# A two-block transformer kernel: the first norm's conditioning by halves of the features, GpSimd's share of the S5 turns, and the first half tile of the gated unit inside S5's last wait

## The reference, cut to what matters

```python
hl = modulate(rms_norm(xl, g_mix_norm[l]), sh1, sc1)      # h * (1 + sc1) + sh1
pl = hl @ wl                                              # 1024 -> 2048: q, k, v, fourier
...                                                       # attention, fourier mix, routed experts
```

```python
u = h @ w_in                                              # 1024 -> 1024
bu = einsum('btgh,gph->btgp', u_blk, b_bar)               # complex, 64 groups x 64 states
_, hs = associative_scan(_s5_combine, (a_elems, bu), axis=1)
y = einsum('btgp,ghp->btgh', hs, c_mat).real + d * u
g = gelu(y)
val, gate = split(g @ w_glu + b_glu, 2)                   # the gated unit, 1024 -> 2048
return val * sigmoid(gate)
```

## Time and profile before

| | us |
|---|---|
| median of 3 runs (2205.2 to 2207.2) | 2206.32 |
| the profiled execution, its own time | 2203.61 |
| its span in the profile | 2201.5 |
| TensorE busy | 2114.5 (96%) |
| VectorE busy | 1220.8 (55%) |
| ScalarE busy | 699.4 (32%) |
| GpSimd busy | 146.0 (7%) |

### The profile page before, as it was taken

One profiled execution on the slowest core, in us unless ns is written; L12 is line 12 of the kernel. 1 busy time (PEld: TensorE's weight loads), 2 busy tenths in 40 slices (PEclk: granted clock), 3 DMA queues, 4 the chain that ended last, 5 costly groups with the idle time before them and its releaser, 6 DMA issues.

```text
span 2201.5 us, 24790 instructions
## 1 busy us (share of the span) xinstructions
PE 2114.5 (96%) x9898; PEld 1424.2 (65%) x9898; DVE 1220.8 (55%) x1749; ACT 699.4 (32%) x1055; POOL 146.0 (7%) x149
## 2 busy tenths in 40 slices
PE   7999898998999899999999999999999999999997
PEld 3444444333333336678888888878777788888886
DVE  1875843344433336896665564576985646343434
ACT  4123422110111107223242232256884424232321
POOL 0011000003300023001000000000110000000000
PEclk9999999999999999999999999999999999999999
DMA  9754355999999992225454545324442222222221
GB/s 389 269 197 143 115 234 199 425 427 425 426 427 426 426 409 89 77 68 203 160 175 160 181 152 181 129 75 126 125 154 77 96 96 77 96 95 95 95 96 57
DMA packets 112679, 433.26 MB, mean 197 GB/s; under 512 B 7854, under 2 KB 13106, under 8 KB 98888
## 3 DMA queue, kind: packets, MB, share of 16 engines
q1 hardware_dynamic: 92872, 360.02, 42.8%
q0 software_dynamic: 19712, 71.93, 9.1%
HBM read 429.13 MB, written 6.36 MB: 198 GB/s over the span
## 4 chain that ended last, share of the span: by engine, by line
PE 59%; PEld 14%; DVE 8%; DMA 7%; issue 6%; ACT 3%; DVEq 2%; SPq 0%; POOLq 0%; PEldq 0%; POOL 0%; ACTq 0%
PE PS L1140 7%; PE PS L752 6%; PE PS L756 6%; PE PS L755 6%; PE PS L852 5%; DMA work<-in_w_dn 4%; PEld PS L752 4%; PEld PS L756 4%; PEld PS L755 4%; PE PS L1163 4%; PE PS L1407 3%; PE PS L1411 3%; PE PS L1410 3%; PE PS L982 2%; PE PS L1177 2%
## 5 line engine op out<-in xcount | busy, mean ns | idle before, releaser
L756 PE MATMUL PS<-work_f32r,work_f32r 128*128 128x512 f32 x1168 | 454.4, 389 | 0.0
L752 PE MATMUL PS<-work_f32r,work_f32r 128*128 128x512 f32 x768 | 299.5, 390 | 2.1 <-DVE work_f32r L2931 1.1
L755 PE MATMUL PS<-work_f32r,ring_f32r 128*128 128x512 f32 x768 | 298.8, 389 | 0.0
L2150 DVE TENSOR_TENSOR ring_f32r<-ring,work_f32r 128x2048 fp32r<-128x2048 f32 x100 | 227.7, 2287 | 125.5 <-ACT work_f32r L1561 125.0
L1561 ACT ACTIVATE work_f32r<-ring 128x2048 fp32r<-128x2048 f32 x100 | 190.3, 1910 | 305.8 <-DMA ring<-in_mlp_w 248.8
L756 PEld LDWEIGHTS PS<-work_f32r,work_f32r 128*128 128x128 f32 x1168 | 219.2, 188 | 45.7
L1140 PE MATMUL PS<-work 128*64 128x512 f32 x752 | 170.6, 597 | 2.2 <-ACT work L1756 2.2
L752 PEld LDWEIGHTS PS<-work_f32r,work_f32r 128*128 128x128 f32 x768 | 144.2, 188 | 33.0 <-DVE work_f32r L2931 1.5
L755 PEld LDWEIGHTS PS<-work_f32r,ring_f32r 128*128 128x128 f32 x768 | 144.2, 188 | 30.1 <-issue 0.2
L752 PE MATMUL PS<-h_f32r,work_f32r 128*128 128x512 f32 x400 | 156.0, 390 | 1.2 <-DVE work_f32r L2170 1.2
L755 PE MATMUL PS<-h_f32r,ring_f32r 128*128 128x512 f32 x400 | 155.6, 389 | 0.0
(11 more groups left out here) (440 smaller groups left out, 3334.8 us busy)
## 6 DMA issues: line engine op xcount, KB each, us to landing
work<-in_w_gu SPq DMA_DIRECT2D x47, 2048.0 KB, 21.2
ring<-in_mlp_w SPq DMA_DIRECT2D x64, 1024.0 KB, 5.2
work<-in_w_dn SPq DMA_DIRECT2D x24, 2048.0 KB, 24.4
ring<-in_w_gu SPq DMA_DIRECT2D x16, 2048.0 KB, 23.9
work<-in_ada_w_2T POOLq DMA_DIRECT2D x16, 1536.0 KB, 6.8
ring<-in_m_w_in SPq DMA_DIRECT2D x20, 1024.0 KB, 5.2
work<-in_w_adaT POOLq DMA_DIRECT2D x8, 2048.0 KB, 10.7
work<-in_ada_w_2T POOLq DMA_DIRECT2D x32, 512.0 KB, 3.6
```

What stands on the lines that cost most here:

```text
L752: mm = nc.tensor.matmul(PS[:, bank + k, :], f32r(w_of), f32r(hi(c)), start=first and c == 0, stop=False)
L755: nc.tensor.matmul(PS[:, bank + k, :], f32r(wlo), f32r(hi(c)), start=False, stop=False)
L756: mm = nc.tensor.matmul(PS[:, bank + k, :], f32r(w_of), f32r(lo(c)), start=False, stop=last and c == 3)
L2150: tt(f32r(ring[:, s, at, :]), ring[:, s, at, :], f32r(tiles[s][:, at, :]), ALU.subtract).then_inc(w_split, 1)
```

## The change

It has three parts.

**Front.** The columns of `w_ada` are reordered outside the kernel, so that one part of 2 MB holds four row chunks of one half of the features (shift and scale). SyncE's order becomes: part 0, part 1 (first half of the features), half the projection tile, part 2, part 3, the other half. TensorE conditions the first half of the features, turns it, starts the projections chunk by chunk with four of them side by side, and does the conditioning of the second half between chunks. The first norm's sum is joined on VectorE (`add_square`) and needs two chunks on TensorE. One `modulation` and two evacuations move ahead.

**S5.** VectorE keeps the doublings n = 1 to 8; GpSimd does n = 16 (two calls), then 32 and 64 for one quad at a time, with a semaphore for each quad. VectorE takes two of the four lag copies. TensorE's order gets turns of powers between the projections and loses four `keep_warm` calls.

**Gated unit.** The first half tile (48 matmuls) is issued in pieces around `states_to_outputs(7)`, and its weights are split on VectorE ahead of quad 7.

```diff
@@ SyncE, front
-            for q in range(4):
-                sp.dma_start(w_early[q], rows(A["w_ada"])[:, 2 * q:2 * q + 2, :]).then_inc(in_mod[q], 16)
-            load_tile(0, 0, 0, columns(A["w_in"]))
+            for q in range(4):
+                load_early(q)
+                if q % 2:
+                    half = q // 2
+                    sp.dma_start(ring[:, 0, 4 * half:4 * half + 4, :], rows(A["w_in"])[:, 4 * half:4 * half + 4, 0:TN]) \
+                        .then_inc(tile_loaded[half], 16)
@@ relay
-                    sp.wait_ge(bu_and_t_mm, 2 * (k - 1))
+                    sp.wait_ge(bu_and_t_mm, within_in(k - 2))
@@ GpSimd
-            pool.wait_ge(mod_mm, 1)
+            pool.wait_ge(mod_mm, COND)
+            pool.wait_ge(in_mod[3], 16)
...
+            def turn_doubled(n, first, count):
...
+                for k in range(2):
+                    ptt(dst[k], turn_c[:, part, 0:n], by[k], ALU.mult)
+                    ptt(made[k], turn_s[:, part, 0:n], by[1 - k], ALU.mult)
+                pool.drain()
+                ptt(dst[0], dst[0], made[0], ALU.subtract)
+                pool_step(ptt, dst[1], dst[1], made[1], ALU.add)
+            pool.wait_ge(s5_angles_set, 2)
+            for first in (0, 16):
+                turn_doubled(16, first, 16)
+            for q in range(KC):
+                for n in (32, 64):
+                    turn_doubled(n, 4 * q, 4)
+                pool.sem_inc(s5_set, 1)
@@ TensorE, front
-            norm_sum(0, h, T)
...
+            pe.wait_ge(in_x, 16)
+            keep_warm(3, 10)
+            pe.wait_ge(cond_ready, 1)
+            condition(0)
+            first_norm_sum()
+            keep_warm(3, 4)
+            condition(1)
+            first_spread_out()
+            conditions_turned(0)
+            keep_warm(3, 6)
...
+            for c in range(KC):
+                if c % 4 == 0:
+                    pe.wait_ge(tile_loaded[c // 4], 16)
+                pe.wait_ge(h_ready, c + 1)
+                for e in range(4):
+                    if c == 3 and e == 2:
+                        conditions_turned(1)
+                    mm = nc.tensor.matmul(PS[:, e, :], ring[:, 0, c, e * P:(e + 1) * P], h[:, c, :], start=(c == 0), stop=(c == KC - 1))
...
+                if c == 1:
+                    condition(2)
+                elif c == 2:
+                    condition(3)
             norm_sum(1, csq, CTX)
@@ TensorE, S5
+            s5_project(0)
+            turn_powers(4)
+            s5_project(1)
+            turn_powers(5)
+            inputs_to_states(0)
+            turn_powers(6)
+            s5_project(2)
+            inputs_to_states(1)
+            turn_powers(7)
+            within_chunks(0)
+            states_to_outputs(0)
+            within_chunks(1)
+            for k in range(3, KC):
+                s5_project(k)
+                inputs_to_states(k - 1)
+                within_chunks(k - 1)
+                states_to_outputs(k - 2)
+                outputs_turned(k - 3)
+            inputs_to_states(KC - 1)
+            within_chunks(KC - 1)
+            states_to_outputs(KC - 2)
+            outputs_turned(KC - 3)
+            glu_first((0, 1))
+            states_to_outputs(KC - 1)
+            outputs_turned(KC - 2)
+            glu_first((2,))
+            outputs_turned(KC - 1)
+            glu_first((3,))
+            pe.wait_ge(lo_ready, LOWS["glu"][0] + KC)
+            split_half(SPLITS["glu"], 0, 1, 0, lambda c: glu_hi[:, 4 + c, :], lambda c: glu_lo[:, 4 + c, :], False, True,
+                       None, glu_mm, glu_tiles, False)
@@ ScalarE, S5
                 if k == 0:
                     powers_turned(4)
+                    copy_lags(0)
+                elif k == 1:
                     powers_turned(5)
-                    for a in range(1, 4):
-                        copy_lags(a)
...
                     powers_turned(6)
+                    copy_lags(1)
...
-                if k == KC:
+                if k == KC - 2:
                     round_half(first, 0, 0, glu_tiles)
+                elif k == KC:
@@ VectorE, S5
-            for power in range(3):
+            for power in range(4):
...
+            for a in range(2, 4):
+                for j in range(S5_J):
+                    for g in range(2):
...
+                last.then_inc(lags_copied, 1)
-            turn_doubled(16, turn_t)
-            last_doublings(0)
             for q in range(KC):
+                dve.wait_ge(s5_set, quads_turned(q))
+                if q == KC - 1:
+                    split_weight_half("glu", 0, 0, 0, glu_tiles)
                 s5_quad(q)
-                if q in (0, 2, 4):
-                    last_doublings(4 * q + 8)
```

## The result

The changed kernel took 2185.36 us (median of 4 runs, 2183.96 to 2188.26) where the kernel before, on the same chip, took 2205.76: a ratio of 0.991, 95% interval 0.9898 to 0.9922, or 20.4 us less by the medians (17.2 to 22.5 by the ratio's interval). The forecast was 17.0 less, 2189.3.

What follows compares the result with a forecast made beforehand. Loads of some 13 MB bound the front and VectorE's pace (14.5 us a quad) bounds S5. 4.3 + 18.5 - 4.8 - 1.0 = 17.0 us less, 2189.3; range 2182.5 to 2199.

Steps and rivals of the forecast that it cites:

- the 6 named: End of S5: of 18.5 us less, 6 come from gated-unit matmuls that fill TensorE's last wait.
- Front: Conditioning and first projections: the new load order starts projections at 27.0 instead of 36.62; 4.3 us less, ends 3.0 and 4.9.
- both gains pass through whole: Behind front and S5: no gain is lost, since waits are between engines and on signalled transfers, none on a fixed time.
- S5 without collisions: S5 to the first gated tile's end: 995.4 against 1013.9, 18.5 us less, 12 of them VectorE's doublings taken off.
- The start 0.7 late for n = 8: Start of S5: s5_project(0) begins 0.7 us later because doubling n = 8 stands ahead of the copy of the statistics.
- Collisions: S5's quads: VectorE and GpSimd block each other on SBUF, pace 13.5 us or more; 4.8 us late in all.
- the 0.75 of an operation of 1.04: Earlier trace at 1652.81: VectorE waited some 0.75 us on a GpSimd product of 1.04; given for charging over half an operation.
- Clock in S5: S5's last waits: TensorE's clock falls without four keep_warm calls and costs 1.0 us.
- The first: S5: no collisions that matter, GpSimd runs ahead and its operations fit into gaps; 22.8 us less, 2183.5; chance 0.20.
- The second: S5: strict alternation, a whole GpSimd operation before each of VectorE's; some 2196 to 2198; chance 0.20.
- The third: S5: GpSimd starves VectorE if it needs more than 17 us a quad; 2213 at 18 a quad; chance 0.04.
- rivals 1, 2 and 4: 1 and 2: no collisions that matter, strict alternation, 0.20 each; 4: the front gives nothing, 2193.6, 0.06.

Runs made afterwards that it cites:

- dve_turns: The changed kernel with the turn doublings n = 16, 32, 64 back on VectorE, where they stood before; 2200.99 us, ratio 0.9978.
- no_fill: The changed kernel with the gated unit's first half tile whole behind the last turned outputs instead of in S5's last waits; 2191.9 us, ratio 0.9946.
- front_only: The kernel before with the new front alone, S5 and the gated unit as before; 2201.89 us, ratio 0.9987.
- one_table: The changed kernel with GpSimd making one quad's table for all eight quads, idle from some 870 us, numbers wrong; 2186.07 us, ratio 0.9913.
- s5_only: The kernel before with the new S5 and the gated unit's first half tile alone, front as before; 2188.01 us, ratio 0.9929.
- tail: The changed kernel with the weight split ahead of quad 6 and gated-unit columns ahead of the last two quads' outputs; 2180.96 us, ratio 0.9884.

## Why the prediction came out as it did

The time, 4 us under the forecast, lies in its range, but steps of the sum were off in opposite directions, so that it lies as near as it does is partly luck.

- **What bounds it.** Right. Taking the doublings off VectorE moved state 8 by 14 us (dve_turns), filling the last wait gave 5.5 in the trace and 6.5 to 7.9 in the times (no_fill) against the 6 named.
- **Front, 4.3 forecast.** 3.74 at the second tile in the trace of after, 3.2 on average over twelve: the order and the hidden loads held, and part 1 ran at the higher clock. Off were the start of the first projection (0.75) and the length of what follows it (0.65). The step that failed is the sentence that both gains pass through whole, "the waits there are between engines and on transfers". They are, but TensorE's clock falls in them, from execution to execution at other places, and in front_only a transfer took 1.2 longer: in the profiled execution of after the experts' slow group alone took 2.4 of the 3.7, in that of front_only all was gone by 228. On average 2.9 us are left at the end (front_only), with 0.9 to 4.9, so that something is lost is seen in single traces, and how much on average stays open.
- **S5 without collisions, 18.5 forecast.** From the first projection to state 8 the forecast is 117.3 and the trace 118.5: the rounds took 0.4 more, the last projection with its inputs 0.6, and 0.2 lie in other places. The start 0.7 late for n = 8 was about right (0.4 to 0.5 behind the experts).
- **Collisions, 4.8 forecast.** This is the most mis-sized term; on the path they cost 0 (one_table). The pace was put at 13.5 and more in six quads because every one of nine operations was charged at least half of a GpSimd operation, 2.2 a quad. Measured are 1.4 to 2.0 in five quads, since GpSimd does most of the waiting (872 ns for 404), and TensorE's slack of 1.65 a round, which the prediction had in hand, holds that with the sixth quad's help. The 4.8 itself is a choice and not a sum: the 0.75 of an operation of 1.04 that it names would, by its own steps, give a pace of 14.5 and some 9.6. The row that it leaned on the earlier trace rows had a VectorE operation behind one long GpSimd operation; the small ones of the doublings mostly stood behind VectorE's.
- **The Trainium skill's rules.** That a VectorE instruction with two SBUF inputs and a GpSimd instruction that reads SBUF block each other (Trainium skill, SBUF — State Buffer, Who interferes with whom) is borne out by the 0.69 that became 1.26. The section lets the order of issue decide who blocks; it has no price for two rows of small operations, and how the waiting is shared out between them decided the term. The estimate of 5.0 us a quad from the cost of a two-input operation (Trainium skill, GPSIMD Engine Reference, 3.1 Elementwise) was too low, the 7.0 from rows was near the 6.7 measured without collisions.
- **Clock in S5, 1.0 forecast.** Too small: the last group lost 1.7 and the first column 1.0 behind it, some 2.8 on the path (22.1 us for the 19.3 forecast). This differs by execution too: the same stretch took 20.8 in one_table, where the last group took 2.38.
- **The sum.** By these steps the stretch from S5's first projection to the tile's end was to become 13.4 shorter (12.7 and the late start of 0.7) and became 15.3 shorter: 4.8 back for the collisions, 1.8 off for the clock, 1.2 off for the rounds. Of this 0.4 to 0.5 go to the late start, and 0.6 come from a later group, 70 us behind the tile, which both traces with the old S5 show at the lower clock and those of after and s5_only do not. That makes 15.4; s5_only's time says 15.7. The front was to bring 4.3 and brought 2.9. The two misses cancel in part, and the total is better than its terms. The 1.8 between 18.6 for the parts and 20.4 by the medians is within the noise.
- **Rivals.** The first, no collisions that matter, has the right outcome on its own question, at 0.20, and its 2183.5 is 1.9 under the measured median; but its reason, that GpSimd's operations fit into gaps, is wrong: they do stretch VectorE's quads, and the slack of TensorE's round hides it. The second's 2196 to 2198 does not follow from the prediction's own price: 4.5 a quad leaves 1 of S5's gain, and with 3.5 of the front that is some 2202, outside the range. The third was tested and is real at 18.9 us a table. The chances of the outcomes below 2201.9 (forecast and rivals 1, 2 and 4) add up to 0.96, where the prediction gives 0.91.

## What to carry to other kernels

Work given to GpSimd beside VectorE costs the path only what the partner's slack does not hold: add up the stretched quads against the rounds they hide in, and count how much of the blocking each side bears before charging it to VectorE. Time won early in this program reached the end only in part, more in some executions than in others, since TensorE's clock fell in waits of 2 to 4 us. Real work put into such waits (here columns of the next product: 5.5 us in the change, 7.9 more in tail) paid in S5; idle matmuls have to be reckoned with their measured price, and at the experts they were not shown to bring anything.

## What the runs showed of the hardware

- At the waits for the experts' weights every group behind 3.3 to 3.7 us of waiting was slow (8.4 to 10.1 us for 7.09) in all 14 traces, and so was one behind 2.75; four behind 2.8 to 3.1 and all behind 2.2 and less were not. Elsewhere the same wait of 2.36 was followed by a group of 8 matmuls in 1.56 us in six traces and in 1.9 to 2.9 in eight.
- GpSimd and VectorE do not share a collision evenly: products of 128 elements went from 404 to 872 ns on GpSimd, while VectorE's quads with nine operations that collide grew by 1.4 to 2.0 of some 11 us; in all GpSimd took 27 us longer and VectorE 8.5. Under a steady row of 256-element products a quad grew by 2.5 to 2.9.
- An idle fp32 matmul of 128x128 took 0.225 us, two instructions in the trace.
